# Moving the weight-slot signals of TensorE, and one head's transposes, in a two-layer decoder kernel

## The reference, cut to what matters

```python
mem_k, mem_v = mem @ mem_wk, mem @ mem_wv
for layer in range(2):
    mix = even_mixer(x, ...) if layer == 0 else odd_mixer(x, ...)   # 0: convolution + sparse attention; 1: gated short convolution
    x = layer_norm(ALPHA * x + mix)
    q = x @ wq                                   # 4 heads of 256
    p = softmax(q @ mem_k.T / 16)                # per head
    x = layer_norm(ALPHA * x + (p @ mem_v) @ wo)
    # group = argmax of 4, then the top 2 of its 8 experts, gated
    x = layer_norm(ALPHA * x + sum(gate * (silu(x @ w1[e]) * (x @ w3[e])) @ w2[e]))
```

## Time and profile before

| | |
|---|---|
| median of 3 runs | 1376.88 us (1374.98 to 1380.55) |
| profiled execution, its own time | 1377.9 us |
| its span | 1376.1 us |
| TensorE matmul busy | 1142.7 us (83%) |
| chain that ended last, shares | PE 58%, DMA 31%, SyncE's queue 6%, issue 3% |
| moved from and to HBM | 477.39 MB, mean 347 GB/s |

### The profile page before, as it was taken

The page is one execution under the profiler, slowest core; times in us unless marked ns, Lnnn a source line. Parts: engine busy times, 40 slices in busy tenths (PEclk is TensorE's granted clock), DMA queues, the critical chain, the costliest instruction groups (busy, mean ns, idle before and its releaser), DMA issues.

```text
span 1376.1 us, 30241 instructions
## 1 busy us (share of the span) xinstructions
PE 1142.7 (83%) x11896; PEld 735.4 (53%) x11897; DVE 393.5 (29%) x1032; ACT 165.3 (12%) x462; POOL 30.5 (2%) x85
## 2 busy tenths in 40 slices
PE   8999999997996776768799999999896766766656
PEld 7885658554554344335458867655453433434333
DVE  1972632351331221212232133253231111111213
ACT  1112502110110000000010001111110000000001
POOL 3000000000000000000000000000000000000001
PEclk9999999998998898888999999999998888888888
DMA  9856059579999999999997657555999999999996
GB/s 347 253 184 245 1 179 370 216 308 428 428 428 430 428 429 427 431 428 428 428 409 276 245 200 324 204 220 202 425 428 428 430 428 427 429 428 430 427 429 273
DMA packets 69241, 477.39 MB, mean 347 GB/s; under 512 B 8460, under 2 KB 13868, under 8 KB 43852
## 3 DMA queue, kind: packets, MB, share of 16 engines
q1 hardware_dynamic: 67148, 470.27, 83.3%
q0 software_dynamic: 2048, 6.47, 1.4%
HBM read 473.58 MB, written 3.15 MB: 346 GB/s over the span
## 4 chain that ended last, share of the span: by engine, by line
PE 58%; DMA 31%; SPq 6%; issue 3%; another core or an unknown queue 1%; DVE 1%; ACT 0%; POOL 0%; DVEq 0%
DMA ring<-in_moe_w_dram 21%; PE bank L1073 13%; PE bank L588 12%; DMA slot<-in_moe_w_dram 10%; PE bank L611 8%; SPq L500 5%; PE bank L1091 4%; PE bank L1099 3%; PE bank L1056 2%; PE bank L596 2%; PE bank L797 2%; PE bank L957 1%; PE bank L975 1%; PE bank L645 1%
## 5 line engine op out<-in xcount | busy, mean ns | idle before, releaser
L1073 PE MATMUL bank<-ring,xT 128*32 128x256 f32 x1920 | 174.5, 447 | 40.1 <-DMA ring<-in_moe_w_dram 40.1
L1634 DVE SCALAR_TENSOR_TENSOR xT<-xT,bank 64x256 f32<-64x256 f32 x73 | 30.3, 415 | 491.8 <-ACT xT L1900 491.7
L1073 PE MATMUL bank<-slot,xT 128*32 128x256 f32 x1120 | 167.4, 465 | 2.9 <-issue 2.9
L1073 PE MATMUL bank<-held,xT 128*32 128x256 f32 x608 | 93.8, 470 | 57.3 <-DMA slot<-in_moe_w_dram 48.6
L588 PE MATMUL bank<-xT,ring 128*128 128x256 f32 x640 | 139.9, 379 | 0.7 <-PE bank L588 0.7
L1073 PEld LDWEIGHTS bank<-ring,xT 128*32 128x32 f32 x1920 | 89.9, 128 | 80.3 <-issue 60.0
L588 PEld LDWEIGHTS bank<-xT,ring 128*128 128x128 f32 x640 | 121.1, 190 | 17.3 <-issue 1.1
L1073 PE MATMUL bank<-spare,xT 128*32 128x256 f32 x512 | 76.7, 466 | 46.2 <-DMA ring<-in_moe_w_dram 45.0
L611 PE MATMUL bank<-ring,slot 128*128 128x512 f32 x256 | 111.4, 593 | 0.7 <-PE bank L588 0.7
L1073 PE MATMUL bank<-gains,xT 128*32 128x256 f32 x512 | 75.3, 459 | 42.2 <-DMA slot<-in_moe_w_dram 42.2
L1091 PE MATMUL bank<-ring,xT 128*32 128x256 f32 x1824 | 108.9, 379 | 0.0
(11 more groups left out here) (292 smaller groups left out, 1113.3 us busy)
## 6 DMA issues: line engine op xcount, KB each, us to landing
ring<-in_moe_w_dram SPq DMA_DIRECT2D x94, 2048.0 KB, 47.2
slot<-in_moe_w_dram SPq DMA_DIRECT2D x44, 2048.0 KB, 48.8
held<-in_moe_w_dram SPq DMA_DIRECT2D x16, 2048.0 KB, 41.3
spare<-in_moe_w_dram SPq DMA_DIRECT2D x14, 2048.0 KB, 47.0
gains<-in_moe_w_dram SPq DMA_DIRECT2D x14, 2048.0 KB, 47.1
ring<-in_od_w_in_dram SPq DMA_DIRECT2D x6, 2048.0 KB, 21.3
ring<-in_xa_wq_dram SPq DMA_DIRECT2D x4, 2048.0 KB, 11.4
ring<-in_xa_wo_dram SPq DMA_DIRECT2D x4, 2048.0 KB, 12.7
```

Of the source, the lines that this page charges most:

```text
L1073: ins = mm(b1[qs[2 * m + h], 0:S], xg[:, k, :], ws[m][:, k, h, :, :], start=(k == 0), stop=(k == KC - 1))
L1634: stt(out=glu, in0=th, scalar=1.0, in1=banks[5][0:P // 2, 0:S], op0=ALU.add, op1=ALU.mult).then_inc(fam.glu_done, 1)
```

## The change

The calls that signal a used slot are moved behind a later group of products. Each is the same wait and the same `nop`; none is added and none taken away. The output projection signals `a` ahead of (1,1) instead of behind it, and `b` from its callers. In the cross-attention `xattend(3)` stands ahead of `xweigh(2)` instead of behind it.

```diff
-            def out_projection(name, i, ready):
+            def out_projection(name, i, ready, between=None):
...
                         filled(ins, ("f", i, t, h))
+                        if between is not None and t + h == 0:
+                            between()
                         if t == 1 and h == 0:
                             turned(("n", i), x, 0)
-                    if t == 1:
-                        signal_release(f"{name}a", ("f", i, 1, 0))
-                        signal_release(f"{name}b", ("f", i, 1, 1))
+                            signal_release(f"{name}a", ("f", i, 1, 0))
...
-            signal_release("av", ("a", CC - 1))
-            release(pe.nop(), "ag")
...  (behind the two transposes of "cols")
+            signal_release("av", ("a", CC - 1))
+            release(pe.nop(), "ag")
...
-            signal_release("q", ("q", 1))
...
+                if b == 0:
+                    signal_release("q", ("q", 1))
...
-            signal_release("kv", ("v", TT - 1))
-            release(pe.nop(), "kw")
...
                     ins = by_weight(None, wkey, ((2 * j + c) % 4) * P, memT, ps[:, c * S:(c + 1) * S], 512)
+                    if j == 0 and c == 0:
+                        signal_release("kv", ("v", TT - 1))
+                        release(pe.nop(), "kw")
+                    if j == 2 and c == 0:
+                        signal_release("mk0", ("mk", 1))
                 filled(ins, ("mk", j))
-                if j % 2:
-                    signal_release(wkey, ("mk", j))
...
             filled(ins, ("cvar",))
+            signal_release("mk1", ("mk", 3))
...
             filled(ins, ("ch",))
-            signal_release("c0", ("ch",))
-            release(pe.nop(), "c1")
...
             memory_values(0, 0)
+            signal_release("c0", ("ch",))
+            release(pe.nop(), "c1")
...
             memory_values(1, 0)
-            signal_release("mv0", ("mv", 1, 0))
...
             filled(ins, ("c2",))
+            signal_release("mv0", ("mv", 1, 0))
...
+            def mixer_released(h):
+
+                signal_release(f"od_c{h}", ("odb", 4 * h + 3))
+                release(pe.nop(), f"od_h{h}")
+                release(pe.nop(), f"od_b{h}")
...
                             by_weight(None, f"od_c{h}", c * P, xT, pss[c][:, 0:S], 512)
+                            if h == 1 and c == 0:
+                                mixer_released(0)
...
-                        signal_release(f"od_c{h}", ("odb", 4 * h + 3))
-                        release(pe.nop(), f"od_h{h}")
-                        release(pe.nop(), f"od_b{h}")
...
-                out_projection(f"wo_mix{L}", 3 * L, (mixed_first, mixed_second)[L])
+                out_projection(f"wo_mix{L}", 3 * L, (mixed_first, mixed_second)[L], (None, lambda: mixer_released(1))[L])
...
                     by_tile(3 * L, f"xq{L}0", c * P, early[0][:, c * S:(c + 1) * S], 0)
+                    if c == 0:
+                        signal_release(f"wo_mix{L}b", ("f", 3 * L, 1, 1))
...
-                signal_release(f"xq{L}0", ("xq", L, 1))
...
-                    if j % 2:
-                        signal_release(wkey, ("xq", L, j))
...
                 xscores(0)
+                signal_release(f"xq{L}0", ("xq", L, 1))
...
                 xscores(2)
+                signal_release(f"xq{L}1", ("xq", L, 3))
...
                 xweigh(1)
+                xattend(3)
                 xweigh(2)
-                xattend(3)
                 xweigh(3)
...
                 logits(0)
+                signal_release(f"xo{L}b", ("f", 3 * L + 1, 1, 1))
```

## The result

The changed kernel takes 1368.65 us (median of 5 runs, 1368.28 to 1368.78) against 1376.88 (1374.98 to 1380.55); the ratio is 0.9939, with a 95% interval from 0.9928 to 0.9949. So it is 8.2 us faster, where 9.8 were forecast, and the time lies 1.6 us above the forecast of 1367.1. The profiled execution took 1368.37 us (span 1366.5) against 1377.9 (1376.1): between these two single executions the difference is 9.5.

What follows compares the result with a forecast made beforehand. TensorE was taken to bound the dense parts and the weight stream the expert parts. Gains of 6.0 us in layer 0 and 3.8 in layer 1, together 9.8, took the 1376.9 median to 1367.1; range 1364.0 to 1373.5.

Steps and rivals of the forecast that it cites:

- The bound and the pass-through: TensorE bounds dense parts, the weight stream expert parts; each microsecond the stream starts earlier ends the layer a microsecond earlier.
- The cost of a drain: At a used-slot signal in dense parts: a 0.29 us gap plus 0.24 us for refilling the array, 0.53 in all.
- `kv`: Signals `kv`/`kw`, with six more waits in the same gap: 0.68 gap plus 0.24 filling, 0.92 us gained.
- `mk1` and `c0` with the GELU: Signals ahead of transposes `chT`: 0.53 for `mk1`, and 0.48 for `c0`/`c1` after a GELU wait of up to 0.2 us.
- the mixer halves: Layer 1's two mixer signals: a 0.70 gap plus 0.24 filling each, 1.88 us gained together.
- The new places cost nothing: Moved signals have 8 to 18 matmul records queued, so each wait costs 0; upper bound 0.53 us each.
- `av`/`ag`: Signal with a 0.47 us gap, newly covered only by two short transposes: 0.35 us gained, bounds 0.1 and 0.7.
- `wo_mix0`: Layer 0 mixer output: 0.55 gap plus 0.24 filling, 0.79 us; TensorE reaches tile 1's transposes just after DVE's norm ends.
- `wo_mix1`: Layer 1 plain signal, priced as a gap of 0.28 to 0.32 us plus 0.24 filling.
- `mv0`: Plain memory-value signal, priced as a gap of 0.28 to 0.32 us plus 0.24 filling.
- The heads: Cross-attention's last head: a 0.6 us wait for probabilities replaces the 0.78 copy wait; 0.28 us gained per layer, 0.56 together.
- The `nop` ahead of step 6: In the cross-attention projection's first product, due about 255 us but effective at 250.59: evidence that TensorE's sequencer runs ahead.

Runs made afterwards that it cites:

- layer 1 undone: The changed kernel with all of layer 1's calls, heads included, back in their old places; 1372.46 us, ratio 0.9973 to the kernel before.
- the kernel with the waits: The changed kernel plus 14 waits of TensorE for its own last product, with no added `nop` or transfer; 1375.57 us.
- cut-head kernel: The changed kernel with `xweigh(2)` split around `xattend(3)` and the `av`/`ag` signal moved behind the memory's 16 transposes; 1366.42 us.

## Why the prediction was right, and where its terms were off

**The bound and the pass-through** held. What the dense parts give comes through the expert parts: -0.52 and 0.07 us in the profiled executions, and layer 1 undone confirms it for layer 0: 5.7 of 6.4 us. For layer 1 only the profiled pair shows it.

**The cost of a drain** held: with a `nop` it is 0.29 + 0.24, and where nothing else was late the steps gave this. Between the ends of groups on the two chains: `q` 0.53, `kv` 0.94 (0.92 forecast), `mk0` 0.55, `mk1` and `c0` with the GELU 1.00 (1.01 forecast; a gap of 0.01 is left ahead of the transposes), `xq00` and `xq01` 0.54 each, `xq10` 0.54, `xq11` 0.53, the mixer halves 1.91 (1.88). The split is another than I thought: a bare wait is 0.31, nearly all of it in the group behind it. The `nop`s are more of the rest, but not surely all: in the kernel with the waits one wait with one `nop` is 0.37, not 0.53, and with three 0.69, not 0.94; what makes this difference is open. The Trainium skill, TensorE: Matmul & The Clock Gate, Single matmul latency, has about 0.17 us beyond the streaming, for a single bf16 matmul; the fp32 groups of these runs say 0.24 to 0.27. The sum by that page is 1368.1 (14 x 0.17 is 2.4, not the 2.3 of the forecast, which gave 1368.2), and it is nearer to the median only because other terms fell short.

**The new places cost nothing**, as taken: no issue piece in the middle of a group in either dense part, and one step queued is already enough, where all new places but that of `av`/`ag` have 8 records or more.

**The terms that were too large**, by the chains:
- `wo_mix0` gave 0.47 instead of 0.79 and `wo_mix1` 0.21 instead of 0.53. I wrote that TensorE reaches the transposes of tile 1 as the norm ends, "so this just fits". It was too late by a little: the norm ends at 201.13 (the line below), the products behind (1,1) end at 201.20, and the transposes start at 201.28, in both layers 0.15 us behind the norm's end. So a gap of 0.09 and 0.08 is left, which the chain calls issue, and with it the filling comes back: the eight transposes take 1.13 where they took 0.89. A gap of 0.09 costs 0.33.

```profile
200.32 0.81 DVE L1239 TENSOR_SCALAR x<-x,mv,rstd 128x1024 f32<-128x1024 f32 x1 [1.00 <-POOL rstd L2002]
```

- `av`/`ag` gave 0.20 instead of 0.35: a gap of 0.28 is left, and the transposes behind it fill anew (2.02 for 1.83). The later place in the cut-head kernel removed both.
- `mv0` gave 0.37 instead of 0.53. Behind it stand small products; I had priced their filling like that of a full group.
- The heads gave 0.23 and 0.25 per layer (0.28 forecast), and `xo` 0.01 and -0.02 (0 forecast).

**What the sum did not have** is 1.6 us in layer 0. From the first product of the first head pair's scores to the end of the memory-value steps and the first pieces behind them it is 10.00 us before and 8.41 after, with the same instructions. In the kernel before, 2 us stretches (busy by engine, granted clock, DMA share, GB/s):

```profile
136.00:138.00 2.00, 1.94 (x24) 1.42 (x23) 0.62 (x4) 0.00 (x0) 0.00 (x0) 1.00 0.00 0
138.00:140.00 2.00, 2.00 (x5) 0.86 (x7) 1.43 (x6) 0.40 (x1) 0.00 (x0) 0.51 0.02 4
140.00:142.00 2.00, 2.00 (x7) 0.68 (x4) 1.86 (x7) 0.00 (x0) 0.00 (x0) 0.50 0.00 0
142.00:144.00 2.00, 2.00 (x6) 1.58 (x5) 1.59 (x5) 1.82 (x10) 0.00 (x0) 0.50 0.00 0
```

and in the changed kernel:

```profile
135.00:137.00 2.00, 2.00 (x7) 0.40 (x5) 1.43 (x6) 0.40 (x1) 0.00 (x0) 0.72 0.01 4
137.00:139.00 2.00, 2.00 (x8) 1.56 (x7) 1.90 (x7) 0.08 (x1) 0.00 (x0) 0.50 0.00 0
139.00:141.00 2.00, 2.00 (x11) 1.70 (x10) 1.55 (x5) 2.00 (x11) 0.00 (x0) 0.93 0.00 0
```

The clock stood at its lower level (0.50, 1.2 GHz) for about half as long. With the changed kernel's signals the profiled executions have it both ways: the clock stays at 1.00 here with layer 1 undone, whose layer 0 is that of the changed kernel, and falls for as long as before in the cut-head kernel, whose stretch takes 9.93 us, nearly the 10.00 of before. So I count it to the execution, not to the change; the kernel before was profiled once, so whether it falls that long each time is open. What it costs is not in proportion. From the first pair's scores to the third's it is 12.50 us with layer 1 undone, with no lower clock and the wait of 1.02 for the softmax, 12.99 after and 14.58 before.

Without it the stages give 5.4 and 3.4, 8.8 us in all, and the median moved by 8.2. The forecast's 9.8 was right in mechanism and place, and too large by the terms above, 1.0 us together. That the spans of the two profiled executions differ by 9.6, nearly the 9.8, is luck: 1.6 of it is this stretch.

## What to carry to other kernels

Where an engine waits for its own last product only to tell another that a buffer is free, put the signal one step later: here one step of 0.43 us hid the whole 0.53, and a whole group was not needed. Price a wait by the group behind it as well as by its gap: a gap of 0.09 us cost 0.33. And before a transpose is moved ahead of a product, look when its input is written; here the wait only changed its place until half a product was put on each side.

## What the runs showed of the hardware that I had not expected

The first 64 products (L645) end at 22.84 us before and 23.17 after, but at 25.76 with the cut head and at 26.04 with the waits alone, although nothing ahead of them differs. In the chain of the cut-head kernel they take 16.10 us, in that of the kernel before 14.08:

```profile
9.66 16.10 PE bank L645 x64
```

Of the 2.9 us between these two, 0.9 is a later first product (9.66 for 8.76), and the products themselves take 2.0 more, at a granted clock of 1.00 in both; what holds them up is open. This 3 us is as large as some of the effects looked for. It lies ahead of every change made here, so stages have to be compared from behind it, and the spread of the kernel before (1374.98 to 1380.55) may well come from there; only one execution of each kernel was profiled, so that is not shown.

The `nop` ahead of step 6 took effect when the sequencer reached it, not when the products written ahead of it had run: SyncE's transfer behind it went out at 250.59, 0.7 us into a product whose step 6 was due at about 255. The Trainium skill, Advanced Engine Details and Errata, Sequencer Loop, has engine instructions pushed into a queue, where they wait, while control instructions start executing. It doesn't say there which of the two a `nop` is. As an engine instruction it would have waited; the trace decides against that.
